# Three query tiles of the first layer move from plain f32 to split matmuls, and the conditioning sums around them are dealt anew

## The chip, the cores and the metric
One core of a Trainium2 chip runs the whole program. The metric is the device time of one execution in microseconds, from runs on that core; the profile is of one further execution.

## The reference, cut to what matters
Two layers act on 256 tokens of width 2048, all in float32:
```
mod = silu(c) @ w_ada[l] + b_ada[l]             # 6 vectors of 2048: sh1 sc1 g1 sh2 sc2 g2
h   = rmsnorm(x, norm_g[l,0]) * (1 + sc1) + sh1
u, q, kc, vc, ks, vs, kw, vw, gl = split(h @ w_in[l])
x   = x + g1 * (concat[pool_mixer(u), nsa_mixer(q, ...)] @ w_out[l])
h2  = rmsnorm(x, norm_g[l,1]) * (1 + sc2) + sh2
x   = x + g2 * ((silu(gate) * up) @ w_down[l])    # gate, up = split(h2 @ w_gate_up[l])
```
The weights of w_in, w_out, w_gate_up and w_down are read once, and so is w_ada (2048 x 12288 a layer, some 200 MB in all), whose product with one vector gives `mod`. The change touches where q is computed in layer 0 (h times 1024 columns of w_in) and when pieces of `mod` are summed.

## The kernel before, in words
**Weight tiles.** A layer is a row of tiles numbered t. A tile is four blocks of 128 rows by 512 columns (1 MB), loaded on SyncE's queue into one of four raw buffers, tile t into raw t % 4, and the load of t + 4 waits for `raw_free` of that buffer. Tiles 0 to 11 are the key and value columns, 12, 15, 17, 18 the first query chunk and 20, 22, 23, 25 the second (line 36), 26 to 34 the pooling columns, then w_out to 51 and the MLP from 52. Tiles in `DIRECT` (13, 14, 16, 19, 21, 24, 32, 37) are small operands used as they are.

**Two ways to multiply.** In split form (`tile`, line 628) ScalarE copies a half of the raw tile, two blocks, to `w_hi` in fp32r (`split_hi`, line 1209), VectorE writes raw minus w_hi to `w_lo` (`split_lo`, line 1624), and TensorE makes three passes for each half of the tile: h_hi with w_hi, h_lo with w_hi, h_hi with w_lo, of four matmuls each over the two token blocks. So TensorE needs a hi half to begin and the lo half after eight matmuls. There are four buffers of hi halves and four of lo halves. In unsplit form (`unsplit`, line 724) TensorE multiplies raw f32 weights by f32 activations, eight matmuls for a tile, and needs nothing of the other engines. Layer 0 is unsplit up to tile 25; `UNSPLIT` is the number of halves that the split form leaves out there. In the profile an f32 matmul has two records. The f32 activations of layer 0 are `xT`, which lies in the buffer `x_sb` that later holds the residual x.

**Periods.** ScalarE and VectorE run one `period(t, nxt)` for each tile that is not DIRECT, in program order (lines 1411 and 2028). In it they split the tile `nxt` and do the attention's small steps. VectorE ends the period with `conditioning(t)`, the conditioning sums dealt to tile t:
```
if nxt is not None: split_lo(nxt, 0)
...
if nxt is not None: split_lo(nxt, 1)
...
conditioning(t)
```
In period 18 VectorE also scales the first query chunk (in the first layer), in period 23 it makes the SiLU of the compressed branch, in 25 the compressed keys.

**Conditioning sums.** w_ada comes in pieces of 128 x 1024 (512 KB), one load each on GpSimd's queue, in a fixed order (`ada_order`, line 170). VectorE multiplies a piece by silu(c) and adds along the row in one instruction (`ada_sums`, line 1634). `ROOM` (line 183) says how many of them each tile gets. A sum frees its buffer, and GpSimd then issues the load of the next piece for that buffer (`load_ada`, line 547). Which buffers are in the ring at a tile is told by `EARLY_RINGS` (line 213): five up to tile 25, then four more, numbers 11 to 14, that lie in `x_sb`. `NEW_AT` (line 254) names the tile at which the loads into newly lent buffers begin. At tile 26 GpSimd waits until TensorE has done with xT, that is until the last unsplit tile's matmuls are counted.

Of the kernel before, what the change touches and what calls it, by code (L numbers as in the profile page):

```python
# [35 lines left out]
T_Q0, T_Q1 = (12, 15, 17, 18), (20, 22, 23, 25)  # L36
T_GL, T_CMP1, T_CMP2 = 13, (14, 16, 19, 21), 24
T_U0, T_POOL, T_PASS2, T_MLP = 26, (32, 37), 44, 52
# [14 lines left out]
def half_of(t):  # L53

    return 2 * (t - sum(d < t for d in DIRECT))
# [4 lines left out]
    return BLK * KT if t == T_GL else 2 * DH if t == T_CMP2 else 1792 if t in T_POOL else 4 * COLS  # L60


UNSPLIT = half_of(T_U0)
RAW_AFTER = {1: 6, 2: 8, 3: 14, 12: 60}
HALVES = half_of(TILES)
PART_HALVES = 2 * PART_TILES
# [103 lines left out]
def ada_order():  # L170
# [9 lines left out]


ATT_SPLIT = [t for t in range(10, T_MLP) if t not in DIRECT]
ROOM = ({10: 3, 11: 2, 12: 5, 15: 5, 17: 4, 18: 4, 20: 2, 22: 2, 25: 2, 26: 4, 27: 1, 28: 2, 29: 4, 30: 3,
         31: 4, 33: 3, 34: 3, 35: 3, 36: 4, 38: 1, 39: 4, 40: 2, 41: 3, 42: 2, 43: 3, 44: 1, 45: 2, 47: 2, 49: 2} |
        {T_MLP + j: n for j, n in ((0, 1), (1, 1), (2, 2), (3, 2), (4, 1), (5, 2), (6, 2), (7, 2), (8, 1))},
        {4: 1, 5: 2, 6: 1, 7: 2, 8: 1, 9: 2, 10: 2, 11: 1, 12: 2, 15: 2, 17: 1, 18: 1, 20: 1, 22: 2, 23: 1, 26: 1, 27: 2,
         28: 2, 29: 2, 30: 2, 31: 1})
# [2 lines left out]
def ada_schedule():  # L190

    mlp = T_MLP + PART_TILES
    stages = [(0, ROOM[0], 12), (0, {T_MLP + j: 2 + (j in (12, 16)) for j in range(9, 24)}, 4),
              (0, {t: 1 + ((t - mlp) % 3 == 2 or t - mlp in (3, 6, 9, 12)) for t in range(mlp, TILES - 2)}, 16),
              (1, ROOM[1], 4),
              (1, {T_MLP + j: 2 - (j >= 7 and j % 2) for j in range(3, PART_TILES)}, 4)]
    sums, q = {}, FIRST_HALVES
    for layer, room, groups in stages:
        end = q + groups * GROUP
        for t in sorted(room):  # L200
            n = min(room[t], end - q)
            if n:
                sums[layer, t] = range(q, q + n)
            q += n
        assert q == end, "no room"
    assert q == len(ADA)
    return sums
# [2 lines left out]
ADA_SUMS = ada_schedule()  # L210
RING, LATE_RING, LATE_FROM = (0, 1, 2), (3, 4, 5, 7, 0, 1, 2, 6, 8), 45
FIRST_RING = (0, 1, 2, 9, 10)
EARLY_RINGS = ((25, FIRST_RING), (33, FIRST_RING + (11, 12, 13, 14)), (36, (0, 1, 2, 11, 12, 13, 14)),
               (41, (0, 1, 2, 7, 12, 14)), (44, (0, 1, 2, 7)))


# [7 lines left out]
def ada_slots():  # L224
# [4 lines left out]
    for q in range(len(ADA)):  # L229
# [13 lines left out]
        if q == FIRST_HALVES - 1:  # L243
# [8 lines left out]
X_AT = (40, 42, 44, 46)  # L252
X_FREE = [max(q for q, (s, _, _) in enumerate(ADA_SLOT) if s in slots) + 1 for slots in X_SLOTS]
NEW_AT = {t: [q for q, (s, n, before) in enumerate(ADA_SLOT) if q >= FIRST_HALVES and s in slots and (before is None or before < FIRST_HALVES)]
          for t, slots in ((26, (11, 12, 13, 14)), (38, (7,)), (43, (3, 4, 5)), (45, (6, 8)))}
ADA_LATE = min(q for (layer, t), qs in ADA_SUMS.items() if layer == 0 and t >= LATE_FROM for q in qs)
FREED_LATE = {12: (13, 14), 15: (16,), 18: (19,), 20: (21,), 23: (24,), 33: (32,), 38: (37,)}
assert sorted(t for ts in FREED_LATE.values() for t in ts) == sorted(DIRECT)
# [87 lines left out]
def build(nc, x_in, x_turned, stream, w_ada, vec, vec_all, c_row, const, gate_row, out):  # L346
    ctx = ExitStack()
    with ctx:
# [65 lines left out]
        raw_free = [count(f"raw_free{s}", TILES // 4, PART_TILES // 4) for s in range(4)]  # L414
# [9 lines left out]
        gemm_done = count("gemm_done", 2 * HALVES, 2 * PART_HALVES, 8)  # L424
# [114 lines left out]
        @block.gpsimd  # L539
        def _(pool):  # L540
            for q, (s, _, before) in enumerate(ADA_SLOT[:FIRST_HALVES]):
                if before is not None:

                    pool.wait_ge(ada_summed.sem, before + 1)
                pool.dma_start(ada_buf[s], w_ada[q]).then_inc(ada_first[s].sem, 16)

            def load_ada(q):
                s, _, before = ADA_SLOT[q]
                if before is not None:
                    pool.wait_ge(ada_summed.sem, before + 1)  # L550
                pool.dma_start(ada_buf[s], w_ada[q]).then_inc(ada_landed[s].sem, 16)  # L551

            here = Place()
            for q in range(FIRST_HALVES, FIRST_HALVES + len(FIRST_RING)):
                load_ada(q)
            for layer in range(DEPTH):
                here.layer = layer
                for t in range(TILES):
                    if layer == 0 and t == T_U0:

                        pool.wait_ge(gemm_done.sem, gemm_done.start + 2 * UNSPLIT)
                        pool.wait_ge(h_ready.sem, 8)
                    if layer == 0 and t == 38:

                        pool.wait_ge(bank_s.full.sem, bank_s.full.at(here, S_USE["pooled 3"] + 1))
                    if layer == 0 and t == 43:

                        pool.wait_ge(bank_s.full.sem, bank_s.full.at(here, S_USE[f"scores {NSTEP - 1}"] + 1))
                    if layer == 0 and t == 45:

                        pool.wait_ge(bank_b.full.sem, bank_b.full.at(here, B_USE["heads 3"] + 1))
                    if layer == 0:
                        for q in NEW_AT.get(t, ()):
                            load_ada(q)
                    if layer == 0 and t in X_AT:
                        n = X_AT.index(t)
                        cols = slice(n * 512, (n + 1) * 512)

                        pool.wait_ge(x_updated.sem, x_updated.at(here, 2 * n + 2))
                        pool.dma_start(x[:, :, cols], x_in.rearrange("(q p) d -> p q d", p=P)[:, :, cols],  # L580
                                       accum_op=ALU.add).then_inc(x_added[n].sem, 16)
                    for q in ADA_SUMS.get((layer, t), ()):
                        if ADA_NEXT.get(q) is not None:
                            load_ada(ADA_NEXT[q])

        @block.tensor
        def _(pe):
            here = Place()
# [549 lines left out]
            for layer in range(DEPTH):  # L1138
# [7 lines left out]
                for i, t in enumerate((*T_Q0, *T_Q1)):  # L1146
                    if t == 23:
                        hidden_fold()
                        stage_turn(bank_a, A_USE["q 0"], ST_Q0, 0, 4)
                        stage_turn(bank_b, B_USE["q 0"], ST_Q0 + 1, 1, 4)  # L1150
                    attention_side(t)
                    g = i % 4
                    if layer == 0:
                        unsplit(t, chunk(C_Q + i // 4), g, lambda t=t: middle(t))
                    else:
                        tile(t, chunk(C_Q + i // 4), h_rows(g), g == 0, g == 3, lambda t=t: middle(t))
                    if t == 12:
                        gate_logits()
                        kv_turn(1)
                        hidden(0)  # L1160
                    if t == 15:
                        kv_turn(2)
                        hidden(1)
                    if t == 18:
                        hidden(2)
                    if t == 20:
                        hidden(3)
# [16 lines left out]
                for n in range(3):  # L1184
                    for i in range(2):
                        t = T_PASS2 + 2 * n + i
# [19 lines left out]
        def _(act):  # L1206
            here = Place()
# [203 lines left out]
            def period(t, nxt):  # L1411
# [43 lines left out]
                         cv[:, CV["k_gain"]:CV["k_gain"] + 1])  # L1455
                if t == 26:
                    copy_chunk(25, C_Q + 1, lambda tok: bufb[:, tok, :], lambda tok: uc[:, tok * 512:(tok + 1) * 512])
                    if here.layer == 0:
                        act.sem_inc(raw_free[T_Q1[3] % 4].sem, 1)
                if 1 <= m <= NSTEP:  # L1460
                    n = m - 1
                    nk = step_of(n)[4]
# [132 lines left out]
            for layer in range(DEPTH):  # L1595
                here.layer = layer
                if layer == 0:
                    first_norm()
                else:
                    norm(1, 0)  # L1600

                act.dma_start(cv[:], vec[layer]).then_inc(cv_landed.sem, 16)
                for t, nxt in zip(ATT_SPLIT, ATT_SPLIT[1:]):
                    period(t, nxt if layer or nxt >= T_U0 else None)
                norm(2, T_MLP)
                mlp_part(0, PART_UP, PART_G, False)
                for part in range(PARTS - 1):
                    here.part = part
                    mlp_part(1, PART_UP, PART_G, False)
                here.part = None  # L1610
                mlp_part(PARTS, LAST_UP, LAST_G, True)
# [3 lines left out]
        def _(dve):  # L1615
            here = Place()
# [176 lines left out]
            def first_norm():  # L1793
# [30 lines left out]
                low(7)  # L1824
                dve.sem_inc(lo_ready.sem, UNSPLIT)

# [320 lines left out]
            for layer in range(DEPTH):  # L2147
                here.layer = layer
                if layer == 0:
                    first_norm()  # L2150
                else:
                    norm(1, 0)
                for t, nxt in zip(ATT_SPLIT, ATT_SPLIT[1:]):
                    period(t, nxt if layer or nxt >= T_U0 else None)
                norm(2, T_MLP)
                mlp_part(0, PART_UP, PART_G, False)
                for part in range(PARTS - 1):
                    here.part = part
                    mlp_part(1, PART_UP, PART_G, False)
                here.part = None  # L2160
                mlp_part(PARTS, LAST_UP, LAST_G, True)
# [89 lines left out]
```

## Time and profile before
| | |
|---|---|
| median of 3 runs | 2168.3 us (2167.38 to 2169.26) |
| the profiled execution | 2166.22 us |
| its span, first to last instruction | 2164.4 us |
| mean granted TensorE clock | 0.995 |
| TensorE busy | 2123.4 us, 98% |
| VectorE busy | 1550.2 us, 72% |
| ScalarE busy | 985.3 us, 46% |
| bytes moved by DMA | 595.97 MB, mean 275 GB/s |

The profiled execution lies 2.1 us below the median. Times in the rows are from the span's start. PE is TensorE, DVE VectorE, ACT ScalarE, POOL GpSimd, SP SyncE. An idle time in brackets stands before the row's first instruction, with what ended it.

### The profile page before, as it was taken

To read this page: it belongs to the slowest core of one execution; us is meant where nothing else is said; L and a number is where in the kernel's file an instruction comes from. 1 tells how busy PE (TensorE), PEld (TensorE's weight loads), DVE (VectorE), ACT (ScalarE), POOL (GpSimd) and SP (SyncE) were. 2 spreads that over 40 slices of the span, in tenths; PEclk is the share of its full clock that TensorE was granted. 3 is DMA by queue.
4 is the path that set the end of the run, shared out by engine and by line. 5 is a ranking of instruction groups with operands and counts; after the bars stand their busy time and mean duration, and the time that the engine had idled before them with its cause. 6 is when DMAs were issued, how large, how long until landed. Compare 5 with 4: busy or idle time off the path is not lost.

```text
span 2164.4 us, 25299 instructions
## 1 busy us (share of the span) xinstructions
PE 2123.4 (98%) x9624; PEld 1686.7 (78%) x9624; DVE 1550.2 (72%) x2265; ACT 985.3 (46%) x1521; POOL 208.4 (10%) x392
## 2 busy tenths in 40 slices
PE   7899999999999999999999999999999999999999
PEld 3345888788888888888878788878888888888887
DVE  6767998898688887787877774678755555455555
ACT  2123664744344444443465476475434443444443
POOL 3212122111011111111001100001000000000000
PEclk8999999999999999999999999999999999999999
DMA  9999899799598888888757865458755455555554
GB/s 390 412 404 410 309 333 382 296 341 362 205 342 322 322 325 311 313 322 320 292 204 268 328 237 201 156 218 310 298 214 193 181 190 194 195 187 188 191 193 155
DMA packets 112028, 595.97 MB, mean 275 GB/s; under 512 B 12642, under 2 KB 13090, under 8 KB 65188
## 3 DMA queue, kind: packets, MB, share of 16 engines
q1 hardware_dynamic: 55232, 390.83, 48.3%
q0 software_dynamic: 56384, 203.45, 25.2%
q8 instruction: 76, 1.25, 0.2%
q14 instruction: 44, 0.36, 0.0%
q10 hardware_dynamic: 292, 0.09, 0.0%
HBM read 592.18 MB, written 2.13 MB: 275 GB/s over the span
## 4 chain that ended last, share of the span: by engine, by line
PE 87%; DVE 5%; DMA 4%; issue 2%; ACT 2%; SPq 0%; DVEq 0%; ACTq 0%
PE ps L651 78%; PE ps L837 1%; DMA ada<-w_ada 1%; DMA gate<-w_ada 1%; PE ps L963 1%; PE ps L994 1%; PE ps L1099 1%; DVE w_lo L1629 1%; DMA kT<-w_ada 1%; PE ps L1040 1%; PE ps L621 1%; PE ps L616 1%; PE ps L620 1%; DVE ada L1659 1%; DMA k_sb<-const 0%
## 5 line engine op out<-in xcount | busy, mean ns | idle before, releaser
L1629 DVE TENSOR_TENSOR w_lo<-raw,w_hi 128x1024 fp32r<-128x1024 f32 x664 | 797.9, 1222 | 334.9 <-ACT w_hi L1217 334.2
L1217 ACT ACTIVATE w_hi<-raw 128x1024 fp32r<-128x1024 f32 x664 | 693.9, 1057 | 626.2 <-PE ps L651 599.8
L651 PE MATMUL ps<-w_hi,h_hi 128*128 128x512 f32 x1696 | 465.9, 396 | 0.0
L651 PE MATMUL ps<-w_hi,h_lo 128*128 128x512 f32 x1696 | 454.2, 390 | 0.0
L651 PE MATMUL ps<-w_lo,h_hi 128*128 128x512 f32 x1696 | 454.0, 389 | 0.0
L651 PEld LDWEIGHTS ps<-w_hi,h_lo 128*128 128x128 f32 x1696 | 318.4, 188 | 67.4
L651 PEld LDWEIGHTS ps<-w_lo,h_hi 128*128 128x128 f32 x1696 | 318.4, 188 | 67.1
L651 PEld LDWEIGHTS ps<-w_hi,h_hi 128*128 128x128 f32 x1696 | 313.6, 188 | 65.6 <-issue 4.0
L651 PE MATMUL ps<-w_hi,a_hi 128*128 128x512 f32 x848 | 234.4, 398 | 0.0
L651 PE MATMUL ps<-w_hi,a_lo 128*128 128x512 f32 x848 | 226.9, 389 | 0.0
L651 PE MATMUL ps<-w_lo,a_hi 128*128 128x512 f32 x848 | 226.9, 389 | 0.0
L651 PEld LDWEIGHTS ps<-w_hi,a_hi 128*128 128x128 f32 x848 | 157.9, 188 | 36.2 <-issue 4.8
L651 PEld LDWEIGHTS ps<-w_hi,a_lo 128*128 128x128 f32 x848 | 159.2, 188 | 33.6
L651 PEld LDWEIGHTS ps<-w_lo,a_hi 128*128 128x128 f32 x848 | 159.2, 188 | 33.5
L551 POOL DMA_DIRECT2D ada<-w_ada x164 | 86.8, 529 | 768.5 <-DVE half_sum L1659 528.8
L1659 DVE CUSTOM_DVE_ANT_0 ada<-ada,cond,nv 128x1024 f32<-128x1024 f32 x96 | 121.3, 1279 | 23.3 <-DMA ada<-w_ada 12.5
L1659 DVE CUSTOM_DVE_ANT_0 ada<-ada,cond,half_sum 128x1024 f32<-128x1024 f32 x86 | 108.6, 1279 | 11.3 <-DMA ada<-w_ada 11.3
L837 PE MATMUL ps<-raw,x_sb 128*128 128x512 f32 x192 | 88.7, 624 | 21.8 <-ACT x_sb L1344 21.8
L1563 ACT ACTIVATE bufa<-ps 128x256 f32<-128x256 f32 x88 | 33.6, 384 | 164.3 <-PE ps L651 161.7
L2104 DVE TENSOR_TENSOR bufb<-bufa,ps 128x256 f32<-128x256 f32 x84 | 34.0, 421 | 88.9 <-ACT bufa L1563 88.6
L837 PEld LDWEIGHTS ps<-raw,x_sb 128*128 128x128 f32 x192 | 38.3, 202 | 71.0 <-issue 58.8
L2015 DVE TENSOR_TENSOR bufa<-ps,gate 128x512 f32<-128x512 f32 x60 | 38.6, 685 | 50.0 <-PE ps L651 46.6
(239 smaller groups left out, 1600.5 us busy)
## 6 DMA issues: line engine op xcount, KB each, us to landing
raw<-stream SPq DMA_DIRECT2D x360, 1024.0 KB, 5.5
ada<-w_ada POOLq DMA_DIRECT2D x182, 512.0 KB, 7.2
qT<-w_ada POOLq DMA_DIRECT2D x52, 512.0 KB, 8.0
uc<-w_ada POOLq DMA_DIRECT2D x29, 512.0 KB, 7.3
kT<-w_ada POOLq DMA_DIRECT2D x26, 512.0 KB, 7.6
val<-w_ada POOLq DMA_DIRECT2D x26, 512.0 KB, 6.9
pT<-w_ada POOLq DMA_DIRECT2D x26, 512.0 KB, 7.9
gate<-w_ada POOLq DMA_DIRECT2D x26, 512.0 KB, 11.5
```

The source lines that it names most:

```text
L551: pool.dma_start(ada_buf[s], w_ada[q]).then_inc(ada_landed[s].sem, 16)
L616: mm = pe.matmul(bank[:], xh, whi[s][:, k, :], start=begin, stop=False)
L620: pe.matmul(bank[:], xh, wlo[s][:, k, :], start=False, stop=False)
L621: mm = pe.matmul(bank[:], xl, whi[s][:, k, :], start=False, stop=end)
L651: mm = pe.matmul(banks[tok][0][:], rows[2 * a + k][low][:, tok * P:(tok + 1) * P], w[s][:, k, :], start=first and a == 0 and i == 0 and k ...
L837: mm = pe.matmul(bank[:], xT[:, k, tok * P:(tok + 1) * P], raw[t % 4][:, k % 4 * COLS:(k % 4 + 1) * COLS], start=(k == 0), stop=(k == KT - 1))
L1217: act.activation(whi[h % 4][:].rearrange("p k c -> p (k c)"), raw[t % 4][:, a * 1024:(a + 1) * 1024], ACT.Copy).then_inc(hi_ready.sem, 1)
L1563: act.activation(bufa[:, k % 2, tok * 256:(tok + 1) * 256], bank[:, 0:256], ACT.Silu)\
L1629: dve.tensor_tensor(wlo[h % 4][:].rearrange("p k c -> p (k c)"), raw[t % 4][:, a * 1024:(a + 1) * 1024], whi[h % 4][:].rearrange("p k c -> ...
L1659: dve.tensor_tensor_reduce(ada_buf[s], ada_buf[s], cond[:, a * ADA_K:(a + 1) * ADA_K], 1.0, start, ALU.mult, ALU.add, total).then_inc(ada_ ...
L2015: dve.tensor_tensor(buf[:, tok, :], ps[b][:], gate[:, n * 512:(n + 1) * 512], ALU.mult)\
L2104: dve.tensor_tensor(bufb[:, k % 2, tok * 256:(tok + 1) * 256], bufa[:, k % 2, tok * 256:(tok + 1) * 256], ps[b][:, 256:512], ALU.mult).the ...
```

## The change
In layer 0 the tiles 22, 23 and 25 are multiplied in split form as the later ones are; tile 20 stays unsplit. The constant that marks the border, the conditions in the three engines' programs and the releases of buffers follow. The buffers in `x_sb` are lent from tile 22 instead of 26: GpSimd waits there for tile 20's release of its raw buffer. The sums of tiles 20, 22 and 26 are one fewer each, those of 28, 33 and 36 one more each; in the MLP's first part after that the two extra sums move from part tiles 12 and 16 to 14 and 18.
```diff
-UNSPLIT = half_of(T_U0)
+T_SPLIT = T_Q1[1]
+UNSPLIT = half_of(T_SPLIT)
...
-ROOM = ({10: 3, 11: 2, 12: 5, 15: 5, 17: 4, 18: 4, 20: 2, 22: 2, 25: 2, 26: 4, 27: 1, 28: 2, 29: 4, 30: 3,
-         31: 4, 33: 3, 34: 3, 35: 3, 36: 4, 38: 1, 39: 4, ...
+ROOM = ({10: 3, 11: 2, 12: 5, 15: 5, 17: 4, 18: 4, 20: 1, 22: 1, 25: 2, 26: 3, 27: 1, 28: 3, 29: 4, 30: 3,
+         31: 4, 33: 4, 34: 3, 35: 3, 36: 5, 38: 1, 39: 4, ...
...
-    stages = [(0, ROOM[0], 12), (0, {T_MLP + j: 2 + (j in (12, 16)) for j in range(9, 24)}, 4),
+    stages = [(0, ROOM[0], 12), (0, {T_MLP + j: 2 + (j in (14, 18)) for j in range(9, 24)}, 4),
...
-EARLY_RINGS = ((25, FIRST_RING), (33, FIRST_RING + (11, 12, 13, 14)), (36, (0, 1, 2, 11, 12, 13, 14)),
+EARLY_RINGS = ((20, FIRST_RING), (33, FIRST_RING + (11, 12, 13, 14)), (36, (0, 1, 2, 11, 12, 13, 14)),
...
-          for t, slots in ((26, (11, 12, 13, 14)), (38, (7,)), (43, (3, 4, 5)), (45, (6, 8)))}
+          for t, slots in ((22, (11, 12, 13, 14)), (38, (7,)), (43, (3, 4, 5)), (45, (6, 8)))}
...
-                    if layer == 0 and t == T_U0:
+                    if layer == 0 and t == T_SPLIT:
...
-                        pool.wait_ge(gemm_done.sem, gemm_done.start + 2 * UNSPLIT)
+                        pool.wait_ge(raw_free[T_Q1[0] % 4].sem, T_Q1[0] // 4 + 1)
                         pool.wait_ge(h_ready.sem, 8)
...
-                    if layer == 0:
+                    if layer == 0 and t < T_SPLIT:
                         unsplit(t, chunk(C_Q + i // 4), g, lambda t=t: middle(t))
                     else:
                         tile(t, chunk(C_Q + i // 4), h_rows(g), g == 0, g == 3, lambda t=t: middle(t))
...
-                    if here.layer == 0:
-                        act.sem_inc(raw_free[T_Q1[3] % 4].sem, 1)
...
-                    period(t, nxt if layer or nxt >= T_U0 else None)
+                    period(t, nxt if layer or nxt >= T_SPLIT else None)
```

## Rows read from the trace of the kernel before
**Rows 1.** The page: busy time (share) and records; the chain's shares by engine.
```profile
PE 2123.4 (98%) x9624; PEld 1686.7 (78%) x9624; DVE 1550.2 (72%) x2265; ACT 985.3 (46%) x1521; POOL 208.4 (10%) x392
...
PE 87%; DVE 5%; DMA 4%; issue 2%; ACT 2%; SPq 0%; DVEq 0%; ACTq 0%
```
**Rows 2.** Windows: stretch, its length, busy us of each engine, clock, DMA share, GB/s.
```profile
133.00:200.00 67.00, 66.94 (x328) 32.90 (x326) 45.06 (x109) 16.54 (x64) 12.68 (x24) 1.00 1.02 415
```
**Rows 3.** Waits of 133 to 200: total us, times, longest.
```profile
DVE ada L1659 <- DMA ada<-w_ada: 13.7, 7, 4.3
```
**Rows 4.** Timeline of PE, tiles 22, 23, 25: start, us, engine, line, records.
```profile
175.67 7.13 PE L736 MATMUL ps<-raw,x_sb 128*128 128x512 f32 x16
182.64 0.53 PE L918 MATMUL ps<-k_sb,uc 128*128 128x32 f32 x4
...
183.91 7.03 PE L736 MATMUL ps<-raw,x_sb 128*128 128x512 f32 x16
190.78 0.59 PE L963 MATMUL ps<-kT,qT 128*128 128x256 f32 x2
191.21 3.60 PE L736 MATMUL ps<-raw,x_sb 128*128 128x512 f32 x8
194.87 1.08 PE L929 MATMUL ps<-raw,pcT 128*60 128x128 f32 x8
...
199.42 0.38 PE L971 MATMUL ps<-k_sb,bufa 128*128 128x128 f32 x2
```
**Rows 5.** Timeline of PE, tile 26: its first pass, two rows further, its end.
```profile
199.88 1.28 PE L651 MATMUL ps<-w_hi,h_hi 128*128 128x512 f32 x4
...
202.84 1.07 PE L651 MATMUL ps<-w_hi,h_hi 128*128 128x512 f32 x4
...
204.65 1.07 PE L651 MATMUL ps<-w_lo,h_hi 128*128 128x512 f32 x4
205.56 0.38 PE L939 MATMUL ps<-k_sb,pooledT 128*128 128x128 f32 x2
```
**Rows 6.** Timeline of DVE: sums of 17, of 18 (last), of 20; tile 26's lo.
```profile
173.99 1.28 DVE L1659 CUSTOM_DVE_ANT_0 gate<-gate,cond,nv 128x1024 f32<-128x1024 f32 x1 [2.20 <-DMA gate<-w_ada]
...
184.70 1.28 DVE L1659 CUSTOM_DVE_ANT_0 ada<-ada,cond,half_sum 128x1024 f32<-128x1024 f32 x1 [1.24 <-DMA ada<-w_ada]
...
185.99 1.28 DVE L1659 CUSTOM_DVE_ANT_0 gate<-gate,cond,half_sum 128x1024 f32<-128x1024 f32 x1
...
195.15 1.22 DVE L1629 TENSOR_TENSOR w_lo<-raw,w_hi 128x1024 fp32r<-128x1024 f32 x1
```
**Rows 7.** Raw tile 22's issue (timeline), its landing (DMA), tile 26's hi half (ACT).
```profile
166.63 24.66 SPq L502 DMA_DIRECT2D raw<-stream  x6
...
raw<-stream SPq DMA_DIRECT2D x1, 1024.0 KB, 8.5
...
190.72 1.06 ACT L1217 ACTIVATE w_hi<-raw 128x1024 fp32r<-128x1024 f32 x1 [5.79 <-DMA raw<-stream]
```
**Rows 8.** Timeline of PE behind two idle times, and the window behind the second.
```profile
33.23 33.40 PE L837 MATMUL ps<-raw,x_sb 128*128 128x512 f32 x72 [11.20 <-ACT x_sb L1344]
72.00 22.50 PE L837 MATMUL ps<-raw,x_sb 128*128 128x512 f32 x48 [5.37 <-ACT x_sb L1344]
...
72.00:75.00 3.00, 3.00 (x4) 1.45 (x5) 3.00 (x5) 1.07 (x2) 0.98 (x2) 0.50 1.04 414
```
**Rows 9.** Timeline of PE: its two idle times between 200 and 370.
```profile
206.32 0.44 PE L971 MATMUL ps<-k_sb,bufa 128*128 128x128 f32 x2 [0.38 <-ACT kcT L1262]
...
216.53 0.41 PE L971 MATMUL ps<-k_sb,bufa 128*128 128x128 f32 x2 [1.57 <-ACT bufa L1384]
```
**Rows 10.** Timelines of ACT, PE and DVE behind the sums of 33 and before 36's.
```profile
267.24 0.68 ACT L1384 ACTIVATE bufa<-bufa,fac 128x128 f32<-128x128 f32 x2
...
269.25 0.38 PE L971 MATMUL ps<-k_sb,bufa 128*128 128x128 f32 x2
...
284.84 0.87 DVE L1985 SCALAR_TENSOR_TENSOR a_lo<-ps,cv,a_hi 128x256 fp32r<-128x256 f32 x2 [1.62 <-ACT a_hi L1407]
```

More of the change, by code:

```diff
@@ L182 @@
 ATT_SPLIT = [t for t in range(10, T_MLP) if t not in DIRECT]
-ROOM = ({10: 3, 11: 2, 12: 5, 15: 5, 17: 4, 18: 4, 20: 2, 22: 2, 25: 2, 26: 4, 27: 1, 28: 2, 29: 4, 30: 3,
-         31: 4, 33: 3, 34: 3, 35: 3, 36: 4, 38: 1, 39: 4, 40: 2, 41: 3, 42: 2, 43: 3, 44: 1, 45: 2, 47: 2, 49: 2} |
+ROOM = ({10: 3, 11: 2, 12: 5, 15: 5, 17: 4, 18: 4, 20: 1, 22: 1, 25: 2, 26: 3, 27: 1, 28: 3, 29: 4, 30: 3,
+         31: 4, 33: 4, 34: 3, 35: 3, 36: 5, 38: 1, 39: 4, 40: 2, 41: 3, 42: 2, 43: 3, 44: 1, 45: 2, 47: 2, 49: 2} |
         {T_MLP + j: n for j, n in ((0, 1), (1, 1), (2, 2), (3, 2), (4, 1), (5, 2), (6, 2), (7, 2), (8, 1))},
@@ L2153, in _ @@
                 for t, nxt in zip(ATT_SPLIT, ATT_SPLIT[1:]):
-                    period(t, nxt if layer or nxt >= T_U0 else None)
+                    period(t, nxt if layer or nxt >= T_SPLIT else None)
                 norm(2, T_MLP)
```

## The prediction
> **What bounds the kernel now.** I read the page first: its busy line and the chain of waits [rows 1]. TensorE is busy 98% of the span and the chain is 87% PE, so almost every microsecond that TensorE gains or loses is a microsecond of the result, unless a stall elsewhere takes it up. The change sits near 167 to 200 us, so I took the stretch 133 to 200 next [rows 2]: PE 66.94 of 67.00 us busy, VectorE (DVE) only 45.06, and the DMA engines full at 415 GB/s. Two things are at their limit there at once: TensorE, which runs the query tiles as plain f32 matmuls, and the DMA. DVE's free 22 us are no free time for the taking: DVE waits in order for the loads of w_ada whose sums it has to make (13.7 us in seven waits from the ada buffers alone, [rows 3]). Then I took the three timelines of this stretch side by side, PE [rows 4, 5], DVE [rows 6] and the weight tile that ScalarE splits [rows 7]. The reader is to see one fact in them: when TensorE begins tile 22, at 175.67 us, DVE has just ended the last sum dealt to tile 17 (173.99 and 1.28) and still has the four of tile 18 before it, which end at 185.99. It is ten microseconds late, and before the change nothing waits for that, since up to tile 25 TensorE reads raw weights.
>
> **What the change removes: f32 tiles.** Tile 22 goes from 175.67 to 182.64, 6.97 us; tile 23 from 183.91 to 190.78, 6.87; tile 25 from 191.21 to 199.42, 8.21, of which 1.0 is the compressed branch's eight matmuls (1.08 with the tail of the last), so 7.2 [rows 4]. The first split tile, 26, takes 199.88 to 205.56, 5.68 us, in the same company of small matmuls [rows 5]. I take 5.68 for each: the saving on TensorE is 1.3 + 1.2 + 1.5 = 4.0 us.
>
> **What it adds: hi and lo halves.** Three tiles are six halves more for ScalarE (1.06 us each, [rows 7]) and for DVE (1.22, [rows 6]), 7.3 us on DVE against two sums of 1.28 that leave tiles 20 and 22. The order matters more than the amount. In each period both engines run the split of the next tile, and DVE then its sums. So tile 22's lo halves stand in period 20, behind all four sums of period 18.
>
> **Step 1, the hi half.** Raw tile 22 is issued at 166.63 and lands 8.5 us later, 175.1 [rows 7]. ScalarE has waited for it and needs 1.06: TensorE can start at 176.2, 0.5 us later than now.
>
> **Step 2, the lo half.** TensorE has eight matmuls before it needs w_lo: 202.84 to 204.65, 1.81 us [rows 5], so it gets to 178.0. DVE is then in the sums of period 18. Their loads were issued before 176 and no part of the change touches them, so they land as they do: the last one starts at 184.70 and ends at 185.99 [rows 6]. The lo half takes 1.22 more: 187.2. TensorE stands for 187.2 - 178.0 = 9.2 us. Queued behind the wait on TensorE are the rest of tile 22, the fold of the hidden rows, the turns of the queries, and so all of ScalarE's and DVE's later work; nothing runs ahead of it. With the 16 matmuls that are left (four rows of 0.91, [rows 5]) tile 22 ends near 190.9, 8.2 us later than now, the same as 0.5 + 9.2 - 1.3 within 0.2.
>
> **Step 3, the clock.** The trace shows what TensorE does behind a stand of that size [rows 8]. Behind 5.37 us idle the 48 f32 matmul records from 72.00 take 22.50 us; at the full-clock pace of tile 22 (16 records in 6.97, 0.435 each) they would take 20.9, so 1.6 are lost. Behind 11.20 us idle 72 records take 33.40 against 31.3, 2.1 lost. The granted clock is 0.50 in the first three microseconds, the lower of its two levels (1.2 GHz). Bounds: 0, if the clock stays up, and 2.3; between the two rows I take 1.9. The Trainium skill's page "TensorE: Matmul & The Clock Gate", Part 1, says that throttled is the default state and activity releases it; by that rule the clock drops in this stand as well, and without it this step would be 0 and the forecast 1.9 us lower. In 133 to 200 itself no stand shows it.
>
> **Step 4, tiles 23 and 25.** DVE goes on at 187.2 with the second lo half (188.4), the one sum of period 20 (189.7), the two halves of 23 (192.1) and the one sum of 22 (193.4). TensorE, out of tile 22 at 190.9 plus 1.9, wants tile 23's lo after the turns (1.3 us) and eight matmuls, at about 196: covered. ScalarE takes the queries first and then splits 25; its hi halves are there by 197, its lo by 198.2, and TensorE wants them at about 201: covered. Raw tile 26 is asked for when tile 22 nears its end, 192 instead of 183; with 8.5 us it lands at 200 to 201 and is wanted split at about 206: covered, by 3 to 4 us. So the two tiles give their 1.2 + 1.5 and no more.
> Sum at the head of tile 26: +0.5 + 9.2 + 1.9 - 4.0 = +7.6 us.
>
> **Step 5, what is given back.** Between 200 and 370 us TensorE stands twice for the chain DVE bias, ScalarE exp and weigh: 1.57 us at 216.53 and 0.38 at 206.32 [rows 9]. The longer one is behind the four sums of tile 26. DVE reaches that point about 4.4 us later than now (5.6 behind the sums of tile 25, less one sum of tile 26, 1.2), TensorE 7.6 later: both stands vanish, -1.95. Bounds 0 and -1.95; I take the whole.
>
> **Step 6, the other edits, each at nothing.** One sum more at 28, 33 and 36 puts bias and weigh 1.2 us later in the next period. Behind tile 33's sums ScalarE ends the weighing at 267.92 and TensorE takes it at 269.25, 1.3 us of cover, which just holds; before tile 36's, DVE waits 1.62 us for TensorE anyway, so lateness doesn't pile up [rows 10]. Upper bound, all three exposed: 1.2 each, 3.6, less the cover, some 2. Sums moved from part tiles 12 and 16 to 14 and 18 leave tiles in which DVE also turns rows: 0, bounds -0.3 and +0.3, as TensorE shows no idle there. The x_sb buffers lent from tile 22 bring four loads of 512 KB some 10 us earlier; they serve sums of tile 26, which didn't wait; against raw tile 26 they cost at most 2 us of landing, inside step 4's cover.
>
> **Total:** 0.5 + 9.2 + 1.9 - 4.0 - 1.95 = +5.65, say +5.5 us. The profiled execution's own time is 2166.2 (span 2164.4), which gives 2171.7; the median of the runs shown is 2168.3, which gives 2173.8.
>
> **Rivals.**
> (A) DVE is not late at tile 22 and the change gains. What speaks for it: DVE has 22 us free in the stretch, and a few percent more DMA rate would help it. It decides at one point: the end of the sums of period 18. Were they done by 176.8, the stand is gone and the result is +0.5 - 4.0 - 1.95 = -5.4 us, 2162.9. Break-even, without a clock loss, is a stand of 5.45 us, so sums done by 182.2. Against it: 185.99 in the trace with the DMA engines full. The Trainium skill's page "DMA: Bandwidth & Descriptors", section "Where 436 GB/s comes from", puts the fabric's ceiling at 435 GB/s; over the 53 us from 133 an estimate from it is 2.5 us saved at most, a stand of 6.7: still no gain.
> (B) The stand is there and more of it is absorbed: the clock stays up, or drops for one microsecond only. +3.6 us, 2171.9, which is no change within what can be told (0.2% is 4.3 us).
> (C) A second stand: the thicker sums of 28, 33 and 36 show on TensorE, or raw tile 26 comes too late through the early loads. +7.5 to +8, 2176.
>
> **How the numbers follow.** Forecast 0.63, A 0.12, B 0.15, C 0.10. The forecast's own range is +3.8 to +7.5: 2172.1 to 2175.8. Slower by over 0.2% (4.3 us, about what a measurement of this kernel can tell) has C and nine tenths of the forecast: 0.10 + 0.56 = 0.66. Within 0.2%: B and the rest, 0.22. Faster: A, 0.12. The range leaves out A and the tails: 2169.5 to 2178.0.
>
> **What would show it.** Right: a stand of 8 to 10 us on PE that begins near 178 and ends with a w_lo matmul near 187, released by DVE's w_lo, with the granted clock at half behind it; tile 26 beginning 6.5 to 8.5 us later than 199.88; no stand at the place of 216.53; the last sum of period 18 still ending near 186. Step 1 is wrong if ScalarE's first w_hi starts after 176; step 4 if TensorE stands again at 23, 25 or 26. The whole is wrong if DVE's first w_lo starts before 182.

## The result, and the profile after

The changed kernel takes 2176.5 us (median of 5, 2175.6 to 2177.3) against 2168.3 before: ratio 1.0039, 95% interval 1.0027 to 1.005. It is 8.2 us slower. The forecast was 2173.8, and +5.5 for the profiled execution; the profiled execution of the changed kernel takes 2176.1 us with a span of 2174.3, 9.9 us over the span before. One run of the experiments, in the eighth, took 3063.3 us; the median given there counts it, and the other eleven runs have a median of 2166.5.

The page of after, busy time and the chain's shares [rows 1]:
```profile
PE 2123.7 (98%) x9648; PEld 1692.2 (78%) x9648; DVE 1557.1 (72%) x2271; ACT 991.2 (46%) x1527; POOL 209.3 (10%) x392
...
PE 83%; DMA 6%; DVE 6%; issue 3%; ACT 2%; POOL 0%; SPq 0%; DVEq 0%; ACTq 0%; POOLq 0%
```
TensorE's busy time has not fallen, though three tiles are 4 us cheaper; a stretch at half clock gives back part of it, and the rest I did not trace. DVE has 6.9 us more work. The chain has four points less PE and three more of DMA and DVE together.

The timeline of PE after, tile 22 and the heads of tiles 26 and 28 [rows 4, 5, 9]; an idle time stands in brackets before the row, with what ended it:
```profile
175.35 1.15 PE L906 MATMUL ps<-raw,pT 128*32 128x128 f32 x32
177.28 1.20 PE L652 MATMUL ps<-w_hi,h_hi 128*128 128x512 f32 x4 [0.78 <-ACT w_hi L1218]
178.32 1.08 PE L652 MATMUL ps<-w_hi,h_lo 128*128 128x512 f32 x4
188.36 2.08 PE L652 MATMUL ps<-w_lo,h_hi 128*128 128x512 f32 x4 [8.96 <-DVE w_lo L1628]
190.23 1.91 PE L652 MATMUL ps<-w_hi,h_hi 128*128 128x512 f32 x4
191.94 1.21 PE L652 MATMUL ps<-w_hi,h_lo 128*128 128x512 f32 x4
192.99 1.07 PE L652 MATMUL ps<-w_lo,h_hi 128*128 128x512 f32 x4
193.90 0.53 PE L919 MATMUL ps<-k_sb,uc 128*128 128x32 f32 x4
...
208.31 1.28 PE L652 MATMUL ps<-w_hi,h_hi 128*128 128x512 f32 x4
...
223.50 0.41 PE L972 MATMUL ps<-k_sb,bufa 128*128 128x128 f32 x2
```
The first row in the trace before:
```profile
174.59 1.15 PE L905 MATMUL ps<-raw,pT 128*32 128x128 f32 x32
```
Up to here the two executions are 0.76 us apart. They are that far apart at 130 us already, where nothing was changed, so I call it jitter, and shifts below are counted from there. TensorE waits 0.78 us for the hi half, runs eight matmuls and stands 8.96 us for the lo half. The four rows behind it take 5.54 us (188.36 to 193.90), where four rows at full clock take 3.6: 1.9 us for the clock. Windows of after in the stand, behind it and later; columns as in [rows 2]:
```profile
182.00:188.00 6.00, 0.00 (x0) 0.00 (x0) 3.42 (x5) 0.00 (x0) 1.59 (x3) 0.50 1.01 408
188.40:192.00 3.60, 3.60 (x9) 2.83 (x10) 3.60 (x5) 0.00 (x0) 1.06 (x3) 0.50 0.62 225
194.00:200.00 6.00, 6.00 (x35) 5.15 (x34) 2.91 (x6) 3.39 (x5) 0.53 (x1) 1.00 1.01 388
```
The granted clock is at its lower level, 1.2 GHz, in the stand and in the first 3.6 us of work behind it, and back at 2.4 from 194. The DMA rate falls to 225 GB/s there: tile 22's raw buffer is held, SyncE waits for TensorE (its longest wait for it between 160 and 215 us is 16.5), and bytes that were moved in this stretch before have to be moved later.

The timeline of DVE after, from the last sum of tile 17 to tile 25's halves [rows 6]:
```profile
175.04 1.28 DVE L1658 CUSTOM_DVE_ANT_0 gate<-gate,cond,nv 128x1024 f32<-128x1024 f32 x1 [2.45 <-DMA gate<-w_ada]
...
185.88 1.28 DVE L1658 CUSTOM_DVE_ANT_0 ada<-ada,cond,half_sum 128x1024 f32<-128x1024 f32 x1 [1.28 <-DMA ada<-w_ada]
187.09 2.35 DVE L1628 TENSOR_TENSOR w_lo<-raw,w_hi 128x1024 fp32r<-128x1024 f32 x2
189.36 1.28 DVE L1658 CUSTOM_DVE_ANT_0 gate<-gate,cond,half_sum 128x1024 f32<-128x1024 f32 x1
190.56 2.35 DVE L1628 TENSOR_TENSOR w_lo<-raw,w_hi 128x1024 fp32r<-128x1024 f32 x2
192.84 1.28 DVE L1658 CUSTOM_DVE_ANT_0 gate<-gate,cond,nv 128x1024 f32<-128x1024 f32 x1
197.18 2.36 DVE L1628 TENSOR_TENSOR w_lo<-raw,w_hi 128x1024 fp32r<-128x1024 f32 x2 [3.06 <-ACT w_hi L1218]
```
The last sum of tile 18 starts 1.18 us later than before, 0.4 less the jitter, and the lo half of tile 22 comes directly behind it. After that DVE is ahead again; at 194 it waits 3.06 us for ScalarE.

The shift of TensorE's small matmuls against the trace before, less 0.76, goes: head of tile 26 +7.7; 216.5 +6.2; 242 +6.7; 296 +7.7; 326 +8.3; 379 (turns of the second norm) +9.9; 462 +9.0, and it stays there to the end. One stand near the end of w_out is new, PE and, ahead of it, DVE's waits from 340 to 385 (total us, times, longest):
```profile
381.80 0.47 PE L617 MATMUL ps<-w_hi,h_hi 128*128 128x512 f32 x1 [1.74 <-DVE w_lo L1628]
```
```profile
DVE w_lo L1628 <- ACT w_hi L1218: 3.5, 2, 1.8
DVE uc L1658 <- DMA uc<-w_ada: 2.0, 1, 2.0
```
At the same place the kernel before stands 0.52 us, and no load is waited for:
```profile
371.13 0.47 PE L616 MATMUL ps<-w_hi,h_hi 128*128 128x512 f32 x1 [0.52 <-DVE w_lo L1629]
```

### The profile page after: what moved, and what is told of

Read it like the earlier page. It is cut to its first block, busy times and chain, and to the rows that moved or that the text cites. A ratio compares the mean times of both kernels' runs of the same rounds, so it can differ in the third digit from the quotient of the medians.

```text
span 2174.3 us, 25361 instructions
## 1 busy us (share of the span) xinstructions
PE 2123.7 (98%) x9648; PEld 1692.2 (78%) x9648; DVE 1557.1 (72%) x2271; ACT 991.2 (46%) x1527; POOL 209.3 (10%) x392
## 4 chain that ended last, share of the span: by engine, by line
PE 83%; DMA 6%; DVE 6%; issue 3%; ACT 2%; POOL 0%; SPq 0%; DVEq 0%; ACTq 0%; POOLq 0%
PE ps L652 76%; DMA ada<-w_ada 3%; DVE ada L1658 1%; PE ps L1100 1%; DVE w_lo L1628 1%; DMA kT<-w_ada 1%; DMA qT<-w_ada 1%; DMA uc<-w_ada 1%; PE ps L995 1%; PE ps L964 1%; PE ps L617 1%; PE ps L622 1%; PE ps L621 1%; DVE x_sb L1658 1%; ACT w_hi L1218 1%
## 5 line engine op out<-in xcount | busy, mean ns | idle before, releaser
L652 PE MATMUL ps<-w_hi,h_hi 128*128 128x512 f32 x1720 | 473.8, 397 | 0.8 <-ACT w_hi L1218 0.8
L652 PE MATMUL ps<-w_lo,h_hi 128*128 128x512 f32 x1720 | 461.5, 390 | 9.0 <-DVE w_lo L1628 9.0
L652 PE MATMUL ps<-w_hi,h_lo 128*128 128x512 f32 x1720 | 460.9, 390 | 0.0
L652 PEld LDWEIGHTS ps<-w_lo,h_hi 128*128 128x128 f32 x1720 | 323.2, 188 | 77.6 <-DVE w_lo L1628 9.4
L652 PEld LDWEIGHTS ps<-w_hi,h_lo 128*128 128x128 f32 x1720 | 323.1, 188 | 68.6
L652 PEld LDWEIGHTS ps<-w_hi,h_hi 128*128 128x128 f32 x1720 | 318.5, 188 | 67.8 <-issue 4.3
```

The lines of the kernel that those rows point to most:

```text
L652: mm = pe.matmul(banks[tok][0][:], rows[2 * a + k][low][:, tok * P:(tok + 1) * P], w[s][:, k, :], start=first and a == 0 and i == 0 and k ...
```

## The experiments

Each ran beside the kernel before on its chip; their times are medians, with the ratio to before.

**1. The sums of tile 18 behind tile 22's split.**
```diff
-... 17: 4, 18: 4, 20: 1, 22: 1, ...
+... 17: 4, 20: 3, 22: 3, ...
```


> The changed kernel with the four sums of tile 18 dealt behind tile 22's split: none at 18, three at 20 and three at 22 in place of 4, 1 and 1. The same work in all, only VectorE's order and the loads' order differ. Theory (order: the loss is VectorE's lo half of tile 22 standing behind sums that wait for their loads): lo of 22 is done at about 180, TensorE stands there 1 to 2 us in place of 9, the clock stays up, tile 26 begins about 3 us earlier than in the kernel before (it began at 199.9) and some of it is lost again at the stand of 216.5. Time 2165 to 2168. Rival (amount: VectorE has no room for six more halves in the first layer, wherever the sums stand): the stand only moves to tiles 23, 25 or 28, and the time stays at 2172 to 2176.

Measured: 2168.5 us, ratio 1.0 (0.9991 to 1.0009), before 2168.4. Timelines of its PE and DVE:
```profile
177.67 1.20 PE L652 MATMUL ps<-w_hi,h_hi 128*128 128x512 f32 x4 [0.93 <-ACT w_hi L1218]
178.71 1.08 PE L652 MATMUL ps<-w_hi,h_lo 128*128 128x512 f32 x4
180.18 1.20 PE L652 MATMUL ps<-w_lo,h_hi 128*128 128x512 f32 x4 [0.39 <-DVE w_lo L1628]
...
198.17 0.38 PE L972 MATMUL ps<-k_sb,bufa 128*128 128x128 f32 x2
```
```profile
178.91 2.35 DVE L1628 TENSOR_TENSOR w_lo<-raw,w_hi 128x1024 fp32r<-128x1024 f32 x2
181.18 1.28 DVE L1658 CUSTOM_DVE_ANT_0 gate<-gate,cond,nv 128x1024 f32<-128x1024 f32 x1
182.38 1.28 DVE L1658 CUSTOM_DVE_ANT_0 ada<-ada,cond,half_sum 128x1024 f32<-128x1024 f32 x1
183.59 1.28 DVE L1658 CUSTOM_DVE_ANT_0 ada<-ada,cond,half_sum 128x1024 f32<-128x1024 f32 x1
```
The same sums and halves, another order, and the stand falls from 8.96 to 0.39 us; the sums no longer wait for their loads either, since those land meanwhile. This shows the cause of the loss at tile 22. It is worth 8.0 us of median. But I had expected 2165 to 2168, and only 2.3 us of the 4 saved are left at the head of tile 26 (198.17 against 199.42, less 1.0 of jitter of this run); of these all are gone by 380. What takes them is the question of the next experiments.

**2. Only tile 25 split**, x_sb lent from 25, sums as before.
```diff
-T_SPLIT = T_Q1[1]
+T_SPLIT = T_Q1[3]
...
-pool.wait_ge(raw_free[T_Q1[0] % 4].sem, T_Q1[0] // 4 + 1)
+pool.wait_ge(raw_free[T_Q1[2] % 4].sem, T_Q1[2] // 4 + 1)
```


> One third of the change alone: only tile 25 in split form, x_sb lent from 25, all sums dealt as before. Order theory: the two sums of tile 22 end at 193.5, tile 25's first lo half at 194.8, TensorE wants it at 193.0: a stand near 1.8 us against 1.5 saved, no loss of clock; VectorE is then 2.3 us later at the stand of 216.5, which grows from 1.6 to 3 or 4. Time 2169.5 to 2171.5. Amount theory: a third of the whole change's +8.2 us, 2171, without a stand at tile 25.

Measured: 2171.1 us, ratio 1.0014 (1.0005 to 1.0023). Its PE has two stands in tile 25:
```profile
195.93 1.20 PE L652 MATMUL ps<-w_lo,h_hi 128*128 128x512 f32 x4 [2.01 <-DVE w_lo L1628]
...
198.29 1.68 PE L930 MATMUL ps<-raw,pcT 128*60 128x128 f32 x8 [1.16 <-DVE pcT L1897]
```
The first is the one worked out, 2.0 for 1.8. The second I had missed: the compressed branch's SiLU stands behind tile 25's second lo half on DVE, and TensorE wants it in the middle of the tile. The eight matmuls behind it take 1.68 us in place of 1.08 [rows 4]: the granted clock had dropped to 0.50. Behind the first stand, of 2.01 us, it was still 1.00. The wait at the place of 216.5, which I had expected to grow to 3 or 4 us, is 1.29. The time lies within what both theories gave; the stand at the tile speaks for the order.

**3. The changed kernel with the sums dealt as before the change.**
```diff
-20: 1, 22: 1, ... 26: 3, ... 28: 3, ... 33: 4, ... 36: 5 ... (j in (14, 18))
+20: 2, 22: 2, ... 26: 4, ... 28: 2, ... 33: 3, ... 36: 4 ... (j in (12, 16))
```


> The changed kernel with the sums dealt as before the change (2, 2, 4 at 20, 22, 26; 2, 3, 4 at 28, 33, 36; 12 and 16 in the MLP). Order theory: the stand at tile 22 is the same 9 us, since tile 18's four sums are the same, and tile 26 begins as late; the fourth sum at 26 brings a stand of 1 to 1.5 us back at the place of 216.5, the small waits behind 28, 33 and 36 go. Time 2174 to 2177. Rival (the new deal and the lost room behind 28, 33 and 36 make up 3 us of the loss): 2172 to 2174.

Measured: 2175.8 us, ratio 1.0034 (1.0021 to 1.0047), as the changed kernel. Its PE:
```profile
187.88 2.07 PE L652 MATMUL ps<-w_lo,h_hi 128*128 128x512 f32 x4 [8.91 <-DVE w_lo L1628]
...
224.28 0.41 PE L972 MATMUL ps<-k_sb,bufa 128*128 128x128 f32 x2 [1.33 <-ACT bufa L1385]
```
The stand at tile 22 is the same, the wait of 1.33 us behind the fourth sum of 26 is back, and from there to 326 the shift against before doesn't move by 0.1 us. So the small losses of after in that stretch (6.2 to 8.3) are the thicker sums of 28, 33 and 36. The stand at the end of w_out is there too (1.73 us), with DVE waiting 2.1 us for a load, so it isn't the deal's.

**4. The new deal alone, on the kernel before.** The diff's `ROOM` and (14, 18), nothing else.


> The kernel before with the new deal of the sums alone, no tile split more, x_sb lent at 26 as before. Order theory: the deal is worth nothing or a little: the stand of 1.57 us at 216.5 goes, the 0.8 us at 462 go, up to 2 us of small waits behind 28, 33 and 36 come. Time 2166.5 to 2169.5. Rival (the deal itself costs): 2170 to 2172.

Measured: 2166.8 us, ratio 0.9991 (0.9982 to 1.0), 1.7 us under before, with the interval just touching it. Of its PE's waits, the one at 216.5 and this one of the trace before are gone:
```profile
462.19 0.63 PE L1099 MATMUL ps<-k_sb,bufb 128*128 128x128 f32 x4 [0.78 <-DVEq L2102]
```
The shift is -1.9 at 216.5, comes back by 1.3 to 326 and by 0.3 more to 379, and falls by 0.9 at 462. Taken alone, the deal is no part of the loss.

**5. The changed kernel with x_sb lent from 26.**
```diff
-EARLY_RINGS = ((20, FIRST_RING), ...   NEW_AT: ((22, (11, 12, 13, 14)), ...
+EARLY_RINGS = ((25, FIRST_RING), ...   NEW_AT: ((26, (11, 12, 13, 14)), ...
...
-if layer == 0 and t == T_SPLIT:
+if layer == 0 and t == T_U0:
```


> The changed kernel with x_sb's four buffers lent from tile 26 on, as before the change, all else as changed. Theory (ring: lending earlier turns the order in which buffers are used, so that the second sum of tile 47 gets a buffer freed late, its load lands late, VectorE waits 2 us and TensorE 1.7 before the last pair of w_out): the wait on a load near 366 goes, the stand of 1.74 us falls to 0.5 to 0.8. 1 to 1.5 us faster than the changed kernel, 2174.5 to 2175.5. Rival (it is VectorE's lag from 28, 33 and 36 that shows there): the stand stays at 1.5 or more, 2176.5.

Measured: 2175.8 us, ratio 1.0037 (1.0023 to 1.005); against the changed kernel's 2176.5 too little to tell by time. The trace tells it: DVE's waits from 340 to 385,
```profile
DVE w_lo L1628 <- ACT w_hi L1218: 3.5, 2, 1.8
DVE ada L1658 <- DVE x_sb L2001: 0.2, 1, 0.2
```
have no load in them, and TensorE's stand there is 0.13 us, under the 0.5 to 0.8 that I had expected. The whole execution stands 1.9 us later from its first 130 us on. With that taken off, its shift falls by 0.3 between 326 and 379, where that of the changed kernel grows by 1.6. Lending earlier turns the rotation of buffers. Both kernels sum the same piece as the second one of tile 47, and in both it lies in the buffer `uc`. In the changed kernel its load is issued behind the sum of tile 44:
```profile
351.49 0.58 POOL L552 DMA_DIRECT2D uc<-w_ada  x1 [3.83 <-DVE half_sum L1658]
367.83 1.28 DVE L1658 CUSTOM_DVE_ANT_0 uc<-uc,cond,half_sum 128x1024 f32<-128x1024 f32 x1 [1.96 <-DMA uc<-w_ada]
```
In the kernel before, and in this run, it is issued one place earlier, behind the last sum of tile 43. That is at 337.3 in the kernel before, 346.3 with the 9.1 us between the two traces added. So the load starts 5 us later against TensorE's work, and it takes 16.3 us to land in place of 12.6. The price of the early loan, with and without it, is 1.9 us here; between 1 and 8 it is 1.7 by the medians.

**6. One sum from 26 to 46 on the kernel before**, and (14, 18).
```diff
-... 26: 4, ... 45: 2, 47: 2, ...
+... 26: 3, ... 45: 2, 46: 1, 47: 2, ...
```


> The kernel before with one sum moved from tile 26 to tile 46, where VectorE stood 1.75 us before its next split, and with the MLP's two extra sums at 14 and 18. Nothing split more. Theory (a sum costs nothing only where VectorE waits for the split of the next tile): the stand of 1.57 us at 216.5 falls to under 0.4, the 0.78 us at 462 go, and no small waits come behind 28, 33 and 36: 2.0 to 2.5 us faster than before, 2166. Rival (VectorE is full all the way to the MLP, what is taken at 26 is paid at 46): 2167 to 2168.5.

Measured: 2167.4 us, ratio 1.0 (0.9991 to 1.0008), before 2167.8. The small waits stay away, but TensorE stands 1.72 us at 372.8 and DVE waits 1.6 for a load. That load is again the one into `uc`:
```profile
342.90 0.58 POOL L551 DMA_DIRECT2D uc<-w_ada  x1 [3.83 <-DVE half_sum L1659]
```
The sum at 46 has taken a piece and its buffer, so that the first sum of tile 47 gets the buffer that tile 44's sum freed. Its load takes 14.7 us, with the DMA at 381 GB/s, and the piece is wanted at 356.1. The theory that DVE's idle time there is free fails; it had forgotten the load and its place in the rotation. The seven runs in which tile 47 sums a piece that was loaded into `uc` behind tile 44's sum (the changed kernel, 1, 3, 6, 7, 9 and 10) all wait for it, 1.0 to 3.1 us. The five in which that load comes behind tile 43's last sum (the kernel before, 2, 4, 5 and 8) do not.

**7. All of it, dealt by order**, x_sb at 26.
```diff
-... 17: 4, 18: 4, 20: 1, 22: 1, 25: 2, 26: 3, 27: 1, 28: 3, ... 33: 4, ... 36: 5, ... 45: 2, 47: 2, ...
+... 17: 4, 20: 3, 22: 3, 25: 2, 26: 3, 27: 1, 28: 2, ... 33: 3, ... 36: 4, ... 45: 2, 46: 1, 47: 2, 48: 1, ...
...
-(3, 2), (4, 1), (5, 2)
+(3, 2), (4, 2), (5, 2)
```


> Tiles 22, 23 and 25 split, the four sums of 18 behind tile 22's split (three at 20, three at 22), x_sb lent at 26, and the sums that the first experiment put at 28, 33 and 36 put at 46, 48 and part tile 4 of the MLP. Theory (order): tile 26 begins 2 us earlier than in the kernel before, the stand of 216.5 is under 0.5, nothing is given back behind 28, 33 and 36, at most 1 us at the norm behind 379: 3 to 4 us faster than before, 2164.5 to 2165.5. Rival (amount: six halves more are 7 us of VectorE that have to show somewhere before the MLP): 2167 to 2169.

Measured: 2168.1 us, ratio 1.0001 (0.9993 to 1.001), before 2167.8. From 216.5 to 326 TensorE runs a constant 2.3 us ahead (jitter of 0.25 taken off). It loses that, and 1.6 more, by 381, in two stands and the time behind them:
```profile
366.91 0.47 PE L617 MATMUL ps<-w_hi,a_hi 128*128 128x512 f32 x1 [1.06 <-ACT w_hi L1218]
371.87 0.47 PE L617 MATMUL ps<-w_hi,h_hi 128*128 128x512 f32 x1 [1.97 <-DVE w_lo L1628]
```
DVE waits 3.1 us for the load into `uc` ahead of them, as in 6. Behind the second stand the granted clock is 0.50 from 373.3 to 376.3, which costs about 1.5 us more. The expected time was 2164.5 to 2165.5; the time is that of the rival theory, but the trace puts the loss at this one load.

**8. The first experiment with x_sb lent at 26.**


> The first experiment (tiles 22, 23, 25 split, tile 18's sums behind tile 22's split) with x_sb lent at 26 as before the change. Order and ring theory: tile 26 begins 2 us earlier than in the kernel before, less 0.3 to 0.5 us each behind 28, 33 and 36, no wait for a load near 366: 1 to 1.5 us faster than the first experiment, 2166.5 to 2167.5. Rival (amount): no change against it, 2168 to 2169.

Measured: 2166.8 us, ratio 0.9994 (0.9985 to 1.0002), before 2168.4; 1.7 us under the first experiment, as both causes together ask, but not clear of before. In its trace no load is waited for between 340 and 385 and the stand at the end of w_out is gone, where the first experiment stands 1.73 us. Only the loan differs between the two.

**9. The same, with the sums of 33 and 36 at part tiles 4 and 8.**
```diff
-33: 4, ... 36: 5, ... (4, 1), ... (8, 1)
+33: 3, ... 36: 4, ... (4, 2), ... (8, 2)
```


> The same, and the additional sums of 33 and 36 put at part tiles 4 and 8 of the MLP, where the seventh kernel's additional sum at part tile 4 showed no wait. Theory: the small waits behind 33 and 36 go (about 1 us), nothing comes at the norm: 2165.5 to 2166.5, 2 us under the kernel before. Rival (amount): the MLP's first tiles have no room either, 2167.5 to 2169.

Measured: 2167.5 us, ratio 0.9997 (0.9989 to 1.0006), its runs from 2165.0 to 2171.4, a wide spread, where I had expected 2165.5 to 2166.5. The profiled one, 2169.4, shows two losses. One is at tile 22:
```profile
181.98 2.08 PE L652 MATMUL ps<-w_lo,h_hi 128*128 128x512 f32 x4 [3.81 <-DVE w_lo L1628]
```
Its head is that of the eighth kernel, which stands 0.92 us here. In this execution one load of tile 15's sums landed 19.4 us after its issue (16.5 in the others), everything on DVE came 2 us later, and the stand grew to 3.81. So tile 22's split can still be held up by a late load in the better order; whether that makes the spread of the other runs isn't shown. The other loss is at the end of w_out: a stand of 1.92 us at 373.5 with DVE waiting 1.8 for `uc`, as in 6. The two sums moved to the MLP have turned the rotation again.

**10. One sum from 26 to part tile 4 on the kernel before**, and (14, 18).


> The kernel before, nothing split more: one sum moved from tile 26 to part tile 4 of the MLP, the MLP's two extra sums at 14 and 18. Theory: the stand of 216.5 and the one of 462 go and nothing comes for them: 2.2 us faster than before, 2166, as fast as the version with three tiles split within 1 us. Rival: what is taken at 26 is paid at the norm, 2167 to 2168.

Measured: 2166.5 us, ratio 0.9993 (0.9984 to 1.0001), before 2168.4, runs from 2165.5 to 2168.9. The profiled one, 2167.3, has this:
```profile
371.81 0.77 PE L616 MATMUL ps<-w_hi,h_hi 128*128 128x512 f32 x1 [1.98 <-DVE w_lo L1629]
```
DVE waited 1.0 us for `uc` ahead of it, and behind it the granted clock is 0.50. By the times as they stand, this execution is 1.1 us ahead of the one before at 224 and 1.8 behind at 379, so the stand, the clock and the load cost more than the wait at 216.5 gave. The median is nevertheless as low as with three tiles split.

## Why the prediction was right

The mechanism came as forecast; the size was short. The forecast was +5.5 and the median moved by 8.2, to 2176.5, which is over the forecast's own range (to 2175.8) and inside the whole one (to 2178.0). Taken point by point, shifts less 0.76:

- **Step 1, hi half, +0.5:** 0.78 us of waiting and the tile's start 176.5 for 176.2. Right. The sign for a failure of this step was a first w_hi after 176; it started at 176.17, which is 175.4 with the jitter taken off.
- **Step 2, lo half, a stand of 9.2:** 8.96, and 8.91 in experiment 3. The last sum of 18 ended 0.4 later than in the trace before. Experiment 1 moves nothing but these four sums and takes 8.6 us of the stand away, so this is shown.
- **Step 3, clock, 1.9:** 1.9 measured in the four rows behind the stand, with the granted clock at 0.50. Part 1 of "TensorE: Matmul & The Clock Gate" in the Trainium skill states that throttled is the default and activity releases it; this trace agrees, since the first 3.6 us of work behind the stand ran at 0.50. In experiment 1, with 0.39 us of stand, the clock stays at full.
- **Step 4, tiles 23 and 25:** no further stand, all three covers held. DVE waited 3.06 us for ScalarE, as worked out from the queries that it takes first; raw tile 26 was issued at 193.4 and landed at 202.4, its lo half wanted at 210.4. Sum at the head of tile 26: +7.6 forecast, +7.7 measured.
- **Step 5, -1.95:** 1.57 came back (the shift falls by 1.46), the 0.38 stayed. That wait is ScalarE's copy of the turned keys between two steps of TensorE itself; it goes with TensorE and I should not have counted it. 0.4 off.
- **Step 6, the other edits at nothing:** this is the term that was mis-sized. Measured it is +2.8 in place of 0: +2.1 from the thicker sums of 28, 33 and 36 (experiment 3 has none of it, experiment 5 has 2.1, experiment 4 has 1.3), of which my upper bound said "some 2"; +1.6 before the norm from the load that the early loan makes late (experiment 5 has none of it); and -0.9 from (14, 18), for which I had bounds of 0.3. I looked at the loads lent early only as competition for raw tile 26, and not at which buffer each later sum would get. And I counted cover at one place for each sum. Behind tile 33 the shift grows by 0.4 at 266.4, with a wait of 0.17 for DVE's nmax, a step ahead of the 1.3 us of cover that I had looked at, and by 0.1 behind that.

The forecast's sum was +5.65; with step 5 and 6 as measured it is 7.7 - 1.5 + 2.1 + 1.6 - 0.9 = +9.0, the shift of the profiled execution from 462 on. The medians are 8.2 apart, the spans of the profiled executions 9.9 with 0.8 of it jitter. The profiled execution before lies 2.1 us under its median, that of the changed kernel 0.4 under its own, so the two differences agree. Rival C (+7.5 to +8, 2176) lies nearest in time. Of its two ways the thick sums did show, and the early loans did too, but not by raw tile 26, which came in time; what C named came on top of the forecast's stand. Steps 5 and 6 erred by 0.4 and 2.8 us, the same way. Step 6's zero was a guess for the loan and for (14, 18), and 2.8 us is a third of the whole change: that the sum came this near is in part luck. Rivals A and B fall, A by the stand of 8.96, B by the half clock.

What stays open: whether splitting these tiles can win at all. The best with three tiles split (8) and the best without (4, 10) are within 0.3 us, all some 1.6 to 1.8 under before, and only that of 4 has an interval that ends at 1.0 and not beyond. That six halves more cost DVE time that shows elsewhere was the rival theory. It isn't refuted in this milder form: the profiled executions of experiments 1 and 8 are 2.3 and 1.9 us ahead at the head of tile 26, and the medians are 0 and 1.6 us under before; the waits that take the difference have their causes in 28, 33, 36 and in one load. A deal that thickens no sum there and also keeps the load into `uc` behind tile 43's sum was not run: 7 and 9 moved sums away from 33 and 36 and turned the rotation with it. It is the test that would settle this.

## What to carry to other kernels

Before you move a stage to a form that needs another engine, look up how late that engine is at this point of the trace, and not how idle: DVE was idle a third of the stretch and ten microseconds behind. What stands ahead in its queue decides; moving waiting work behind the urgent one was worth 8 us here without changing the amount. And when buffers are lent at another time, or one sum is moved, follow each later use to its buffer and load: the price came 180 us further on, and in six of the ten experiments the same load was late.

## What the runs showed that I had not expected

A load of 512 KB that is issued some microseconds behind four or five others took 14.7 to 19.4 us from issue to landing (experiments 6 and 9), where the median of the loads into the ada buffers is 7.2 in the kernel before and 6.5 in the changed one. So where a sum's buffer stands in the rotation decided here whether DVE waited. And three orders with the three tiles split spread over 6 to 10 us from run to run (9: 2165.0 to 2171.4, 8: 2163.7 to 2171.9, 7: 2164.2 to 2174.0), while the kernel before stays within 4.5; why they do isn't shown.

A stand of about 2 us may or may not bring the clock down. Behind 1.74 us (the changed kernel), 2.01 (experiment 2), 1.72 (6) and 1.92 (9) the granted clock was 1.00; behind 1.97 (7) and 1.98 (10) it was 0.50 for some 3 us and cost about 1.5 us, nearly as much as the 8.96 us at tile 22.
